# Moving the last query products into attention's first row tile, regrouping the weight splits there, and grouping a unit's products in the state space layer

## What is computed

```
h = concat(meta, x)
h += s5_mixer(rmsnorm(h))            # state space layer, gelu, GLU
h += hier_moe(rmsnorm(h))            # 32 experts, top 2
k, v = split(rmsnorm(h, norm_kv) @ w_kv + b_kv)
q = (rmsnorm(h, norm_mix) @ w_q + b_q) * 64 ** -0.5
s = [sink | q @ k_meta | q @ k_band]  # 16 heads of 64, 4 kv heads, window of 128
o = softmax(s) @ [v_meta | v_band]
h += o @ w_o + b_o
h += hier_moe(rmsnorm(h));  out = rmsnorm(h)[16:]
```

## Time and profile before

| what | us |
|---|---|
| median of 3 runs | 2074.23 |
| lowest, highest | 2071.95, 2079.52 |
| the profiled execution: its own time | 2071.16 |
| its span, first to last instruction | 2069.3 |
| PE busy | 1890.1 (91%) |
| DVE busy | 1563.7 (76%) |
| ACT busy | 1248.9 (60%) |

### The profile page before, as it was taken

How to read it: one execution, slowest core, us unless ns; L and a number is a source line. 1 busy time by engine, 2 the same in 40 slices (tenths; PEclk the granted TensorE clock), 3 DMA queues, 4 the chain that set the end, 5 groups by cost and what they waited for, 6 DMA issues and landing times. The chain is left out here.

```text
span 2069.3 us, 30493 instructions
## 1 busy us (share of the span) xinstructions
PE 1890.1 (91%) x10340; PEld 1547.6 (75%) x10340; DVE 1563.7 (76%) x1511; ACT 1248.9 (60%) x1484; POOL 365.6 (18%) x616
## 2 busy tenths in 40 slices
PE   4949999879999999999599999996999999999990
PEld 3638777758888888888498777665788888888880
DVE  8997321489999999999862176646899999999985
ACT  6615321347787778778541076643687788777871
POOL 2000000202212222122224100002122122222114
PEclk9979999999999999999899999998999999999995
DMA  4183400369999999999722020007799999999976
GB/s 107 21 82 125 121 14 0 126 241 367 388 388 378 381 380 380 381 391 385 263 104 69 12 93 1 1 1 269 267 363 371 379 384 390 397 394 391 394 302 254
DMA packets 136168, 504.65 MB, mean 244 GB/s; under 512 B 38610, under 2 KB 68626, under 8 KB 84882
## 3 DMA queue, kind: packets, MB, share of 16 engines
q1 hardware_dynamic: 114786, 468.72, 61.4%
q0 software_dynamic: 18432, 33.86, 4.3%
q10 hardware_dynamic: 2880, 1.12, 0.4%
HBM read 488.47 MB, written 47.32 MB: 259 GB/s over the span
## 5 line engine op out<-in xcount | busy, mean ns | idle before, releaser
L1686 DVE TENSOR_TENSOR moe_lo<-moe_raw,moe_hi 128x2048 fp32r<-128x2048 f32 x378 | 860.5, 2291 | 81.1 <-ACT moe_hi L1552 65.9
L1552 ACT CAST moe_hi<-moe_raw 128x2048 fp32r<-128x2048 f32 x374 | 712.5, 1916 | 127.7 <-PE moe_ps_g L1971 56.7
L1969 PE MATMUL moe_ps_g<-moe_hi,moe_x_hi 128*128 128x512 f32 x512 | 205.9, 402 | 3.1 <-DVE moe_x_lo L1693 3.1
L1969 PE MATMUL moe_ps_y<-moe_hi,moe_h_hi 128*128 128x512 f32 x512 | 204.9, 400 | 3.8 <-DVE moe_h_lo L1813 3.8
L1969 PE MATMUL moe_ps_u<-moe_hi,moe_x_hi 128*128 128x512 f32 x512 | 199.6, 390 | 3.0 <-DVE moe_lo L1686 3.0
L1971 PE MATMUL moe_ps_y<-moe_lo,moe_h_hi 128*128 128x512 f32 x512 | 200.2, 391 | 0.0
L1971 PE MATMUL moe_ps_g<-moe_lo,moe_x_hi 128*128 128x512 f32 x512 | 199.8, 390 | 0.0
L1970 PE MATMUL moe_ps_y<-moe_hi,moe_h_lo 128*128 128x512 f32 x512 | 199.8, 390 | 0.0
L1971 PE MATMUL moe_ps_u<-moe_lo,moe_x_hi 128*128 128x512 f32 x512 | 199.7, 390 | 0.0
L1970 PE MATMUL moe_ps_g<-moe_hi,moe_x_lo 128*128 128x512 f32 x512 | 199.5, 390 | 0.0
L1970 PE MATMUL moe_ps_u<-moe_hi,moe_x_lo 128*128 128x512 f32 x512 | 199.2, 389 | 0.0
(11 more groups left out here) (521 smaller groups left out, 3570.1 us busy)
## 6 DMA issues: line engine op xcount, KB each, us to landing
moe_raw<-moe_w_gate SPq DMA_DIRECT2D x128, 1024.0 KB, 8.4
moe_raw<-moe_w_up SPq DMA_DIRECT2D x128, 1024.0 KB, 9.5
moe_raw<-moe_w_down SPq DMA_DIRECT2D x128, 1024.0 KB, 8.3
mix_r<-ssm_w_glu SPq DMA_DIRECT2D x16, 512.0 KB, 5.6
prj_yc<-y_dram SPq DMA_DIRECT2D x8, 1024.0 KB, 7.2
moe_raw<-y_dram SPq DMA_DIRECT2D x8, 1024.0 KB, 12.6
xn_dram<-moe_work SPq DMA_DIRECT2D x12, 512.0 KB, 5.8
mix_r<-x SPq DMA_DIRECT2D x8, 512.0 KB, 5.7
```

The costliest lines, as they stand in the source:

```text
L1552: A.copy(hi[:, slot(number, k), :], raw[:, k, :]).then_inc(hi_done, 1)
L1686: V.tensor_tensor(lo[:, slot, :], raw[:, k, :], hi[:, slot, :].bitcast(F32), ALU.subtract).then_inc(lo_done, 1)
L1969: T.matmul(out, x_h, w_h, start=first, stop=False)
```

## The change

Three things. First, the state space unit issues the kernel products of both halves together, then all products with the states. Second, q chunks 6 and 7 lose their job for tokens 512 to 1023; these 48 products are done in attention as four blocks of 12 (`late_products`) in the places of the filler products: ahead of step 0 and at the ends of steps 0, 1 and 2. The filler of step 3 goes without replacement. VectorE stores them at the starts of steps 1 and 3 (`store_late`), and SyncE loads b_q again for that. Third, in attention the low parts of the slices that ScalarE casts at the end of step p are made by VectorE in step p + 1, between `keep_own` and `normalize` (those of step 6 at the start of step 7), no longer at the end of step p itself, and `SPLITS` is dealt out anew. Buffers are laid out anew for this: w_o's parts lie over the parts of x, the outputs' parts over those of w_q.

```diff
+N_LATE = 2
@@ outputs(u)
+                out = [[psr[:, 2 * (u % 2) + r, jj * NCH:(jj + 1) * NCH] for r in range(2)] for jj in range(2)]
                 for jj in range(2):
                     j = 2 * u + jj
-                    out = [psr[:, 2 * (u % 2) + r, jj * NCH:(jj + 1) * NCH] for r in range(2)]
                     for r in range(2):
-                        T.matmul(out[r], tm[:, 2 * j + r, 0:P], uc[:, 2 * j + r, :], start=True, stop=False)
+                        T.matmul(out[jj][r], tm[:, 2 * j + r, 0:P], uc[:, 2 * j + r, :], start=(jj == 0), stop=False)
+                for jj in range(2):
+                    j = 2 * u + jj
                     for part, ca in enumerate((ca_re, ca_ni)):
...
@@ projections
     for n in range(K0 + 1, NC):
-        jobs += [(n, *at) for at in HALVES + ((REST,) if n < Q0 else ())]
+        jobs += [(n, *at) for at in HALVES + ((REST,) if n < Q0 else ()) if n < NC - N_LATE or at != HALVES[1]]
@@ phase_attend
-    SPLITS = {0: (0, 1), 1: (2, 3), 2: (4, 5), 3: (6, 7), 4: (8, 9, 10), 5: (11, 12, 13), 6: (14, 15)}
+    SPLITS = {0: (0, 1), 1: (2, 3), 2: (4, 5), 3: (6, 7, 8), 4: (9, 10, 11), 5: (12, 13, 14), 6: (15,)}
...
+            sp.dma_start(bq[:, :], t["b_q"][0].rearrange("(c p) -> p c", p=P), allow_slow_non_contiguous=True).then_inc(bq_in, 16)
...
                 for k in SPLITS[p] if p in SPLITS else ():
                     act.wait_ge(w_in[k % 4], 16 * (k // 4 + 1))
+                    if k == DC:
+                        act.wait_ge(late_mm, N_LATE)
...
+            def low_weights(p):
+                for k in SPLITS[p] if p in SPLITS else ():
+                    dve.wait_ge(w_hi_done, k + 1)
+                    V.tensor_tensor(wo_lo[:, k // DC, k % DC, :], raw[:, k % 4, :], wo_hi[:, k // DC, k % DC, :].bitcast(F32),
+                                    ALU.subtract).then_inc(w_lo_done, 1)
+
+            def store_late(j):
+                dve.wait_ge(late_mm, j + 1)
+                if j == 0:
+                    dve.wait_ge(bq_in, 16)
+                c = DC - N_LATE + j
+                V.tensor_scalar(q_t[:, c, SEQ // 2:], ps_y[:, :], bq[:, c:c + 1], DH ** -0.5, ALU.add, ALU.mult).then_inc(late_free, 1)
...
+                if p == 1:
+                    store_late(0)
+                if p == PAIRS - 1:
+                    store_late(1)
+                    step_values(1)
+                if p == 2 * PAIRS - 1:
+                    low_weights(p - 1)
...
                 if i >= 1:
                     keep_own(p)
+                if p < 2 * PAIRS - 1:
+                    low_weights(p - 1)
                 if p + 1 < NP:
                     normalize(p + 1)
...
-                for k in SPLITS[p] if p in SPLITS else ():
-                    dve.wait_ge(w_hi_done, k + 1)
-                    part = slice(k // DC * HALF, (k // DC + 1) * HALF)
-                    V.tensor_tensor(wo_lo[:, k % DC, part], raw[:, k % 4, :], wo_hi[:, k % DC, part].bitcast(F32),
-                                    ALU.subtract).then_inc(w_lo_done, 1)
...
+            def late_products(j, first, last):
+                if first == 0 and j:
+                    pe.wait_ge(late_free, j)
+                for n in range(first, last):
+                    c, part = n // 3, n % 3
+                    w = (late_hi, late_hi, late_lo)[part][:, j, c, :]
+                    x = t["late_x"][part == 1][:, c, :]
+                    product = T.matmul(ps_y[:, :], w, x, start=(n == 0), stop=(n == 3 * DC - 1))
+                if last == 3 * DC:
+                    product.then_inc(late_mm, 1)
 
             scores(0)
+            late_products(0, 0, 12)
             pe.wait_ge(ident_step, 2)
-            spare_products(12)
...
                 if i >= 1:
                     project(i - 1, c // 4, range(2 * (c % 4), 2 * (c % 4) + 4))
-                else:
-                    spare_products(12)
+                elif p < PAIRS - 1:
+                    late_products(*((0, 12, 24), (1, 0, 12), (1, 12, 24))[p])
```

More of the change, by code:

```diff
@@ L801, in outputs @@
                     pe.wait_ge(gelu_done, u - 1)
+                out = [[psr[:, 2 * (u % 2) + r, jj * NCH:(jj + 1) * NCH] for r in range(2)] for jj in range(2)]
                 for jj in range(2):
                     j = 2 * u + jj
-                    out = [psr[:, 2 * (u % 2) + r, jj * NCH:(jj + 1) * NCH] for r in range(2)]
                     for r in range(2):
-                        T.matmul(out[r], tm[:, 2 * j + r, 0:P], uc[:, 2 * j + r, :], start=True, stop=False)
+                        T.matmul(out[jj][r], tm[:, 2 * j + r, 0:P], uc[:, 2 * j + r, :], start=(jj == 0), stop=False)
+                for jj in range(2):
+                    j = 2 * u + jj
                     for part, ca in enumerate((ca_re, ca_ni)):
                         for r in range(2):
-                            last = T.matmul(out[r], ca[rows[r], j, 1:, :].rearrange("p k c -> p (k c)"),
-                                            st_n[rows[r], 8 * (u // 2) + 4 * part + j % 4, :], start=False, stop=(part == 1))
+                            last = T.matmul(out[jj][r], ca[rows[r], j, 1:, :].rearrange("p k c -> p (k c)"),
+                                            st_n[rows[r], 8 * (u // 2) + 4 * part + j % 4, :], start=False, stop=(part == 1 and jj == 1))
                 last.then_inc(y_mm, 1)
@@ L973, in projections @@
     for n in range(K0 + 1, NC):
-        jobs += [(n, *at) for at in HALVES + ((REST,) if n < Q0 else ())]
+        jobs += [(n, *at) for at in HALVES + ((REST,) if n < Q0 else ()) if n < NC - N_LATE or at != HALVES[1]]
+    t["late_x"] = tuple(x[0][:, 1] for x in (x_hi, x_lo))
     def jobs_to(n):
@@ L980, in split @@
     def split(x, i):
-        return x[0][:, :, i * P:(i + 1) * P] if i < XT else x[1][:, :, :]
+        return x[0][:, i // 4, :, i % 4 * P:(i % 4 + 1) * P] if i < XT else x[1][:, :, :]
     def columns(x, c, at, m):
-        return x[0][:, c, at:at + m] if at < XT * P else x[1][:, c, :]
+        return x[0][:, at // 512, c, at % 512:at % 512 + m] if at < XT * P else x[1][:, c, :]
     def turned(j):
@@ L2051, in ps, with over @@
             return ctx.enter_context(nc.psum_tensor("att_" + name, shape, F32))
+        def over(name, shape, at, dt=F32):
+            return nc.alloc_sbuf_tensor_at("att_" + name, shape, dt, offset=at)
         sem = semaphore_source(nc, ctx, "att_")
@@ L2358, in project @@
                     pe.wait_ge(w_lo_done, DC * half + cs[-1] + 1)
+                if cs[0] == 0 and 2 * i + half == 0:
+                    pe.wait_ge(late_free, N_LATE)
                 if cs[0] == 0 and 2 * i + half and (i, half) != (XT - 1, 1):
@@ L2362, in project @@
                 for c in cs:
-                    oh, ol = o_hi[:, i % 2, c, :], o_lo[:, i % 2, c, :]
-                    wh, wl = (w[:, c, 512 * half:512 * half + 512] for w in (wo_hi, wo_lo))
+                    oh, ol = o_hi[i % 2][:, c, :], o_lo[i % 2][:, c, :]
+                    wh, wl = (w[:, half, c, :] for w in (wo_hi, wo_lo))
                     T.matmul(y, oh, wh, start=(c == 0), stop=False)
@@ L2369, in project @@
                     last.then_inc(y_mm, 1)
-            def spare_products(n):
-                for _ in range(n):
-                    T.matmul(ps_y[:, 0:P], ident[:], ident[:], start=True, stop=True)
+            def late_products(j, first, last):
[8 more added lines that the diff above has]
+                    product.then_inc(late_mm, 1)
             scores(0)
+            late_products(0, 0, 12)
             pe.wait_ge(ident_step, 2)
-            spare_products(12)
             for p in range(NP):
```

57 lines of the change are left out of this document (33 added, 24 removed).

## The result

The changed kernel takes 2062.96 us, the median of 20 runs (lowest 2060.81), where the kernel before, run beside it 20 times, takes 2076.74 (lowest 2071.95). One of the changed kernel's 20 runs took 3310.53 us at a granted clock of 0.591; it is a slow run, and all ratios here compare fast runs with fast runs. The ratio is 0.9942, with a 95% interval of 0.9928 to 0.9956: 12.0 us less, between 9.1 and 14.9. A second series gave 0.9942 again (0.9923 to 0.9961), lowest run 2059.92 against 2071.30. Lowest against lowest the difference is 11.1 and 11.4 us. Forecast were 10.9.

The account below looks back on a forecast made before the run. TensorE was taken as the bound nearly everywhere. Projections -10.9, attention's two row tiles +3.9 and state space units -3.9 sum to -10.9 us, from the median 2074.23 to 2063.3; own range 2061 to 2066, wider range 2057 to 2070.

Parts of the forecast that it names:

- Projections: Projections: two jobs of 24 products go, 48 at 0.227 us each, so 10.9 us less.
- Row tile 0: Attention's first row tile: three late blocks each cost 0.08 us more than a filler, the first block nothing; plus 0.2 us.
- Scores of step 4: Attention, VectorE's ring: with low parts moved out and a store in, these scores come 0.9 us earlier, at 1210.1.
- Loads of w_o: Attention, steps 5 to 7: loads wait for later low parts and delay the scores; the two row tiles lose 3.9 us.
- ScalarE's waits: Attention, a sign: ScalarE waits for w_o before casts in steps 4 and 5, 2 to 4 us each.
- Units: State space units: two fewer changes of row count per unit, at 0.21 us each; 3.9 us less, bounds nothing and 6.7.
- Sum: Whole kernel: 10.9 us less, 2063.3 us counted from the median of 2074.23; chance 0.60.
- hidden case: Rival, attention: loads keep ahead, so the row tiles gain 1.8 us; whole minus 16.6, 2057.6 us; chance 0.13.
- clock rival: Rival, attention steps 4 to 7: pauses drop TensorE to 1.2 GHz, 16 us over four steps; sum +5, 2079.3; chance 0.05.
- clock at full in row tile 1: Attention, a sign: full clock there; a clock row below 0.9 would show the forecast wrong.

Follow-up runs that it names:

- e_best: Changed kernel with six buffers for w_o, low parts on GpSimd and sixteen late products before step 0's transposes; ratio to the kernel before 0.9932, lowest run 2053.88 us.
- e_fillers: Changed kernel plus twelve products of 128 columns that nobody reads before the transposes of steps 4 to 7; ratio to the kernel before 0.9963.
- e_short_loads: Changed kernel with the loads of slices 4 to 15 of w_o cut from 512 to 16 columns; ratio to the kernel before 1.0159.
- e_splits_back: Changed kernel with only the weight splits back in their old place, late products and units kept; ratio to the kernel before 0.9933.
- e_no_units: Changed kernel with only the order of the products in a state space unit undone; ratio to the kernel before 0.9959.
- e_units: Kernel before with only the kernel products of a state space unit put together; ratio to the kernel before 0.9962.
- e_no_late: Changed kernel with all 48 late products back in the projections and the old fillers back in attention's first row tile; ratio to the kernel before 0.9996.
- e_six_slots: Changed kernel with six instead of four buffers for the slices of w_o; ratio to the kernel before 0.9907, lowest run 2056.19 us.
- e_pool_low: Changed kernel with six buffers for w_o and the sixteen low parts formed on GpSimd instead of VectorE; ratio to the kernel before 0.9894.

## Why the prediction was right, step by step

- **Projections, -10.9.** 155.96, 156.50 and 156.46 us with the two jobs, 145.22 to 145.72 without them in six kernels (144.93 in e_best): 10.2 to 11.3, in the middle 10.8. Right. Both profiles of the changed kernel show 147.4, and e_fillers and e_short_loads 147.6: only 8.5 less. There TensorE's clock recovered later at the start of that phase and fell once more further on. The same two stretches, counted from the phase's start, in the changed kernel and in the one before (clock third from the end):

```profile
1031.60:1036.60 5.00, 5.00 (x25) 3.59 (x24) 1.58 (x2) 3.27 (x6) 1.29 (x4) 0.50 0.97 405
1076.60:1096.60 20.00, 20.00 (x108) 17.34 (x106) 8.21 (x19) 3.15 (x3) 13.62 (x6) 0.91 0.20 58
```
```profile
1035.00:1040.00 5.00, 5.00 (x32) 3.88 (x31) 1.59 (x2) 3.28 (x6) 1.27 (x4) 0.66 1.00 418
1080.00:1100.00 20.00, 20.00 (x114) 17.43 (x113) 10.61 (x26) 3.15 (x3) 13.62 (x6) 1.00 0.19 54
```

  e_splits_back has the changed kernel's instructions up to here and took 145.35, so the 2 us do not come from this phase's instructions. Why the clock fell in those four executions stays open.

- **Row tile 0, +0.2.** 0.25.
- **Scores of step 4 earlier by 0.9.** T4 came 0.94 us earlier, 20.51 after T0 where it was 21.45.
- **Loads of w_o.** The order of waits was right, in each of the three steps. On the clock of this profile (11.90 us earlier) the scores of steps 5, 6 and 7 were due at 1204.8, 1213.1 and 1221.5; they came at 1204.65, 1212.85 and 1220.92. From T0 to the scores of step 8 I had 48.5; at full clock it takes 47.9 (1231.35 - 1183.47 in e_no_units), 3.3 more than before instead of 3.9. The term was 0.6 too large, and the 0.6 stands already at the scores of step 7 (1220.92 against 1221.5). ScalarE's waits were 0.7 us in step 3, 2.4 (two together) in step 4 and 2.2 in step 5, at the low end of the 2 to 4 I gave for steps 4 and 5. In the changed kernel's own profile the same stretch takes 49.6 us, 5.0 more than before, with the half clock of step 7 in it.
- **Units, -3.9.** 3.5 in e_units, 3.7 and 3.9 in the changed kernel's two profiles. The 0.21 us for a change of row count was the right price: two fewer made 2.59 into 2.19 and 2.38 into 1.99. The cycle was set by VectorE as expected, 6.33 for 6.3.
- **Sum.** With full clock in attention and the middle of the projections it is -3.6 - 10.8 + 3.3 = -11.1, the difference of the lowest runs. This sum is put together from several kernels' traces. In the changed kernel's own first profile it is -3.7 - 8.5 + 5.0 = -7.2, as the start of the second MoE phase says (7.1 earlier); 1.7 us of the difference are the clock in step 7 and about 2 the clock in the projections. That the fastest executions were spared both is argued from their times, not shown.
- **Luck.** Every term of the sum had the right cause. That the total came within 0.2 us of the lowest runs' difference is in part luck: the loads were put 0.6 us too high, the units 0.3 and the projections 0.1 too high the other way. That 2063.3 meets the median of 2062.96 is luck as well: it was counted from 2074.23, the median of 3 runs, where 20 runs gave 2076.74.
- **Rivals.** The hidden case needed the loads to keep ahead, which six buffers brought about: there it is worth 1.9 us from T0 to T8, forecast 1.8. The clock rival was right in kind: against what I expected, the row of step 7 stood at 0.53. But it covered 3.4 us and not four steps, and cost 1.7. So the sign "clock at full in row tile 1" did not come; at 0.95 the clock stayed above the 0.9 that I had named as the sign of being wrong.

What I didn't see is how the moved splits and the late stores depend on each other. I reckoned the whole against the kernel before, and put it at a loss of 3.9. Without the late stores the move does lose 3.0 (e_no_late against e_units). With them it loses 1.2, because it wins in row tile 0 what the stores would cost there, and one more pair of buffers keeps that gain and takes away the loss in row tile 1.

## What to carry to other kernels

When work is moved later into another engine's gap, follow the buffer it frees: the load behind it moves too, and it comes back through a second engine to the one you watch. Here six buffers, twice the three slices of the fullest step, made the same move worth 5 us more than four. Judge each part of a change beside the others it comes with, by taking single parts out of the finished kernel, since its worth depends on them: here a loss of 3.0 us became one of 1.2.

## What the runs showed of the hardware

- A change between products over 128 rows and over 64 costs TensorE about 0.2 us: the same products took 2.59, 2.38, 2.19 and 1.99 us with four, three, two and one change.
- 256 KB into 128 partitions land 3.0 us after the issue (median), 8 KB after 1.7. Both were issued by SyncE.
- GpSimd's subtraction of 128x512 takes 1.42 us where VectorE's takes 0.60 in a row. Beside it VectorE's product p_own takes 0.98 us on average instead of 0.68 and its product v_step 1.16 instead of 0.41; its other operations stay the same (758 ns for `normalize` in both). First e_six_slots, then e_pool_low:

```profile
L2282 DVE TENSOR_TENSOR att_p_own<-att_pt,att_own_t 128x512 f32<-128x512 f32 x4 | 2.7, 681 | 0.0
L2293 DVE TENSOR_TENSOR att_v_step<-v_sb 128x256 f32<-128x256 f32 x2 | 0.8, 414 | 0.0
```
```profile
L2286 DVE TENSOR_TENSOR att_p_own<-att_pt,att_own_t 128x512 f32<-128x512 f32 x4 | 3.9, 976 | 0.0
L2297 DVE TENSOR_TENSOR att_v_step<-v_sb 128x256 f32<-128x256 f32 x2 | 2.3, 1164 | 0.0
```

- A product in plain float32 of 128 columns takes TensorE about 0.24 us (twelve in 2.84 and 2.94).
- The half clock seems to follow a pause of TensorE but not reliably. It came behind one pause of 2.3 to 2.4 us in two kernels and behind one of 1.65 in a third; behind four pauses of 1.0 to 1.5 us it came in both profiles of the changed kernel (0.53 over 3.6 us of step 7) and in neither of two others with the same row tile. Behind a wait of 2.7 us, ahead of step 0's transposes, it came in none of three kernels (e_six_slots, e_pool_low, e_no_units).
